# Final norm of a decoder block: tiles 0 and 2 scaled by ScalarE and GpSimd, tiles 1 and 3 by VectorE

## The chip, the cores and the metric

The kernel runs on one core of a Trainium2 chip. The metric is the device time of one execution in microseconds (us), the median of several runs. A core has five engines that run their own instruction streams and meet at semaphores: TensorE (PE in the profile, PEld its weight loads), VectorE (DVE), ScalarE (ACT), GpSimd (POOL) and SyncE (SP), which here only issues DMAs.

## The reference

One decoder layer over 512 tokens of width 1024: token mixers, a cross-attention, and a mixture of 32 experts of which each token uses two. Everything ahead of the last step is unchanged here. What matters is how the block ends:

```
for e in range(N_EXPERTS):
    gate, up = jnp.split(t @ w_gate_up[e], 2, axis=-1)
    y = (jax.nn.silu(gate) * up) @ w_down[e]
    out = out + combine[:, e:e + 1] * y
x = x + out
return x * lax.rsqrt(mean(x * x, axis=-1) + EPS) * final_norm
```

## The kernel before

The 512 tokens are four tiles of 128 rows (`NT = 4`), the 1024 columns lie in the free dimension. The experts run one after the other, bound by their weights and by TensorE. The rows of the first 30 experts are written to memory and gathered back by GpSimd (`gpsimd_last`, indirect DMAs into `y1` and `y2`); VectorE adds them, weighted, to the block's input (`rows_in`, lines 2464 and 2465, into `sums`). The last two experts don't take that way: TensorE adds their rows (`late_rows`, line 2448) and then `sums` (`own_rows`, line 2453) in PSUM. Tile t has PSUM banks 2t and 2t + 1, 512 columns each (`sum_banks`). All eight banks are in use then, and none is used again.

What follows, for each tile in turn, is the final norm, the subject of this case:

- ScalarE (`scalar_last`) squares both banks with a running sum (line 2491, one ACTIVATE and one short read of the accumulator for each bank), adds the two halves (line 2494), and takes Ln and Exp (lines 2496 and 2498): a first value `rf` of the root.
- VectorE (`vector_last`) waits for that value (semaphore `sq_done`), refines it in four small operations of one element per partition, each waiting for the one before (`newton`, lines 157 to 160), and then for each bank does `y2 = bank * rf * final_g` in one scalar_tensor_tensor (line 2481). After the second it raises `done`.
- SyncE (`sync_last`) waits for `done` tile by tile, in the order 0, 1, 2, 3, and issues one store of 512 KB for each (line 2442). At the end it waits for all four.

The final norm's weight `final_g`, spread over the partitions, was loaded long before. In the profile `final_g` and the squares' scratch have the name weights_2down, `y2` has the name weights_1lo, `y1` weights_0down and `sums` ring, since they reuse buffers of the weights. GpSimd has nothing to do after the last gather.

Of the kernel before, what the change touches and what calls it, by code (L numbers as in the profile page):

```python
# [10 lines left out]
ACT = mybir.ActivationFunctionType  # L11
AX = mybir.AxisListType

P = 128
SEQ, D, MEM = 512, 1024, 256
NT, MT, KC = SEQ // P, MEM // P, D // P
# [138 lines left out]
def newton(dve, st, r, a, mean, eps):  # L155

    st.link(dve.tensor_tensor(a, r, r, ALU.mult))
    st.link(dve.scalar_tensor_tensor(a, mean, eps, a, ALU.add, ALU.mult))  # L158
    st.link(dve.tensor_scalar(a, a, -0.5, 1.5, ALU.mult, ALU.add))  # L159
    st.link(dve.tensor_tensor(r, r, a, ALU.mult))  # L160
# [1688 lines left out]
def buffer_of(g, e, part):  # L1849

    return g["chunks"][chunk_at(e, part) % BUFFERS]
# [47 lines left out]
def expert_phase(nc, psum, g):  # L1899
# [6 lines left out]
    with ExitStack() as ctx:  # L1906
# [70 lines left out]
        with ExitStack() as inner:  # L1977
# [276 lines left out]

            summed = sem("rows_summed")
            last = finish_phase(nc, psum, g, locals(), inner)
            rows_in, sums = last["rows_in"], last["sums"]
            over = overflow_pass(nc, psum, g, locals(), inner)
# [130 lines left out]
def finish_phase(nc, psum, g, v, ctx):  # L2389

    x_rows, eps, R = g["x_rows"], g["eps"], g["routing"]
    y_dram, y_stored = v["y_dram"], v["stored"]

    def sb(name, shape, dt=F32):
        return ctx.enter_context(nc.sbuf_tensor(name, shape, dt))

    def sem(name):
        return ctx.enter_context(nc.semaphore(name))

    y1, y2 = buffer_of(g, NE - 3, "lo"), buffer_of(g, NE - 3, "hi")  # L2400
    sums = buffer_of(g, NE - 4, "down")
    spare = buffer_of(g, NE - 2, "lo")
    final_g, sqf = spare[:, 0], spare[:, 1]
    ss, lnf, rf, af = (sb(n, [P, NT]) for n in ("ss", "lnf", "rf", "af"))
    ss_half = sb("ss_half", [P, NT, 2])
    got = [sem(f"rows_back{t}") for t in range(NT)]
    summed = v["summed"]
    g_landed, sq_done, done, stored, pe_summed = (
        sem(n) for n in ("g_landed", "sq_done", "fin_done", "out_stored", "pe_summed"))
    EARLY_ROWS = NE - LATE  # L2410

    def sum_banks(t):
        return [psum[2 * t + n] for n in range(2)]

    def gpsimd_last(pool):
        def rows_of(table, rows):
            for t in range(NT):
                for y, row in zip((y1, y2), rows):
                    pool.indirect_dma_start(out=y[:, t, :], out_offset=None, in_=table,
                                            in_offset=bass.IndirectOffsetOnAxis(ap=row[:, t:t + 1], axis=0)  # L2420
                                            ).then_inc(got[t], 16)

        pool.wait_ge(v["longest_set"], 1)
        longest = pool.value_load(R["longest"][0:1, 0:1], min_val=0, max_val=SEQ - 1)
        pool.wait_ge(v["table_steps"], v["TABLE"])
        pool.wait_ge(v["gu_mm"], EARLY_ROWS)
        for q in range(2):
            pool.wait_ge(y_stored[q], 16 * (EARLY_ROWS // 2))
        rows_of(y_dram[:, :], (R["row_1"], R["row_2"]))
        with pool.If(longest >= SLOTS):  # L2430
            pool.wait_ge(v["over_stored"], 32 + 32 * (SEQ // SLOTS - 1) * NE)
            pool.wait_ge(summed, NT)
            rows_of(v["y_over"][:, :], v["over_row"])

    def final_gain(sp):
        sp.wait_ge(v["dn_mm"], EARLY_ROWS)
        sp.dma_start(final_g, g["final_norm"].partition_broadcast(P)).then_inc(g_landed, 16)

    def sync_last(sp):
        for t in range(NT):  # L2440
            sp.wait_ge(done, t + 1)
            sp.dma_start(g["out"][0].rearrange("(n p) d -> n p d", p=P)[t], y2[:, t]).then_inc(stored, 16)
        sp.wait_ge(stored, 16 * NT)

    def tensor_last(pe):
        def late_rows(t):
            for n, bank in enumerate(sum_banks(t)):
                pe.matmul(bank[:], v["late_turned"][n][:, t], v["late_yy"][n], start=True, stop=False)  # L2448

        def own_rows(t):  # L2450
            pe.wait_ge(summed, t + 1)
            for n, bank in enumerate(sum_banks(t)):
                pe.matmul(bank[:], g["ident"][:], sums[:, t, n * 512:(n + 1) * 512], start=False, stop=True).then_inc(pe_summed, 1)  # L2453
        pe.wait_ge(v["late_got"], 2 + LATE)
        pe.wait_ge(v["y_got"], NE)
        for t in range(NT):
            late_rows(t)
        for t in range(NT):
            own_rows(t)

    def rows_in(dve, k, weight, base, landed, signal):
        for t in range(NT):
            dve.wait_ge(got[t], landed)
            k.link(dve.scalar_tensor_tensor(y1[:, t], y1[:, t], weight[0][:, t:t + 1], base[:, t], ALU.mult, ALU.add))
            dve.scalar_tensor_tensor(sums[:, t], y2[:, t], weight[1][:, t:t + 1], y1[:, t], ALU.mult,
                                     ALU.add).then_inc(signal, 1)

    def early_rows(dve):
        dve.wait_ge(v["dn_mm"], NE - 3)
        rows_in(dve, Steps(dve, v["table_steps"], 1, v["TABLE"] + 1), v["early_weight"], x_rows, 32, summed)  # L2470

    def vector_last(dve):
        k = Steps(dve, v["table_steps"], 1, v["TABLE"] + 1 + NT)
        dve.wait_ge(g_landed, 16)
        for t in range(NT):
            dve.wait_ge(sq_done, 5 * t + 5)
            c = slice(t, t + 1)
            newton(dve, k, rf[:, c], af[:, c], ss[:, c], eps[:, 0:1])
            for n, bank in enumerate(sum_banks(t)):
                half = slice(n * 512, (n + 1) * 512)  # L2480
                last = dve.scalar_tensor_tensor(y2[:, t, half], bank[:], rf[:, c], final_g[:, half], ALU.mult, ALU.mult)  # L2481
            last.then_inc(done, 1)

    def scalar_last(act):
        act.wait_ge(v["dn_mm"], EARLY_ROWS)
        for t in range(NT):
            c = slice(t, t + 1)
            for n, bank in enumerate(sum_banks(t)):
                act.wait_ge(pe_summed, 2 * t + n + 1)

                act.activation(sqf[:, n * 512:(n + 1) * 512], bank[:], ACT.Square, scale=D ** -0.5,  # L2491
                               accum_out=ss_half[:, t, n:n + 1]).then_inc(sq_done, 1)
            act.wait_ge(sq_done, 5 * t + 2)
            act.activation(ss[:, c], ss_half[:, t, 0:1], ACT.Identity, bias=ss_half[:, t, 1:2]).then_inc(sq_done, 1)
            act.wait_ge(sq_done, 5 * t + 3)
            act.activation(lnf[:, c], ss[:, c], ACT.Ln, bias=eps[:, 0:1]).then_inc(sq_done, 1)
            act.wait_ge(sq_done, 5 * t + 4)
            act.activation(rf[:, c], lnf[:, c], ACT.Exp, scale=-0.5).then_inc(sq_done, 1)

    return dict(sync=sync_last, tensor=tensor_last, scalar=scalar_last, gpsimd=gpsimd_last, vector=vector_last,  # L2500
                final_gain=final_gain, early_rows=early_rows, rows_in=rows_in, sums=sums)

# [36 lines left out]
```

## Time and profile before

| | us |
|---|---|
| median of 3 runs | 1259.28 (1259.16 to 1260.41) |
| the profiled execution's own time | 1260.81 |
| its span, first to last instruction | 1259.1 |
| start of the first row sum that closes a bank (PE line 2453) | 1243.75 |
| start of the last store's issue | 1256.05 |

Times in rows are from the span's start. The span and the execution's own time differ by 1.7 us, which lies around the instructions. Busy times are shares of the whole span, though the change touches only its last 12 us or so.

### The profile page before, as it was taken

The numbers are of one execution on the slowest core, as the hardware profiler recorded it, in microseconds if no ns is written. First come the engines' busy times: TensorE is split into PE (matmuls) and PEld (weight loads), VectorE is DVE, ScalarE is ACT, GpSimd is POOL, SyncE is SP. The second block draws the span as 40 slices with busy tenths as digits, with TensorE's granted clock in tenths as the row PEclk, the third lists the DMA queues.
The fourth block names the chain that finished last, engine by engine and source line by source line (L and its number), as shares of the span: only waits on it lengthen the run. The fifth ranks groups of instructions, "written<-read, shape, count | busy, mean of one in ns | idle before, by whom it ended". The sixth has DMA issues, their size and how long they took to land. (4 is left out here: it accounts for less than half of the span.)

```text
span 1259.1 us, 18398 instructions
## 1 busy us (share of the span) xinstructions
PE 1232.0 (98%) x7153; PEld 857.5 (68%) x7153; DVE 678.6 (54%) x1228; ACT 384.9 (31%) x979; POOL 401.3 (32%) x431
## 2 busy tenths in 40 slices
PE   8999999999999999999999998999999999999996
PEld 6788989898888989878686786354444535353532
DVE  2744989999998998772534234321213122222126
ACT  2033745546373735522022231111111111111113
POOL 3266765757484753325411210000000000000002
PEclk9999999999999999999999998999999999999999
DMA  9672211221121212322334346889999999999995
GB/s 352 256 292 76 84 68 52 68 85 68 51 70 49 85 61 88 122 104 102 134 135 167 115 193 263 342 359 429 426 429 427 427 426 428 426 426 428 427 382 201
DMA packets 37302, 287.10 MB, mean 228 GB/s; under 512 B 6524, under 2 KB 6652, under 8 KB 23520
## 3 DMA queue, kind: packets, MB, share of 16 engines
q1 hardware_dynamic: 31488, 273.69, 53.9%
q0 software_dynamic: 3552, 8.20, 1.8%
q10 hardware_dynamic: 2176, 4.03, 0.9%
q8 instruction: 58, 0.95, 0.3%
q14 instruction: 28, 0.23, 0.0%
HBM read 269.84 MB, written 19.92 MB: 230 GB/s over the span
## 5 line engine op out<-in xcount | busy, mean ns | idle before, releaser
L2224 DVE TENSOR_SCALAR ee<-ee 128x256 f32<-128x256 f32 x32 | 9.4, 293 | 297.5 <-ACT ee L2121 297.5
L2200 POOL DMA_INDIRECT expert_out<-yy,row_at x30 | 29.4, 982 | 430.3 <-ACT yy L2105 430.3
L1942 PE MATMUL bank<-select,x_rows 128*128 128x256 f32 (+1 forms) x576 | 117.0, 363 | 2.8 <-DVE select L2210 2.8
L1942 PEld LDWEIGHTS bank<-select,x_rows 128*128 128x128 f32 x576 | 100.8, 196 | 21.0 <-issue 7.3
L704 PE MATMUL bank<-h_sums,ring 128*128 128x256 f32 x384 | 92.2, 383 | 0.0
L704 PEld LDWEIGHTS bank<-h_sums,ring 128*128 128x128 f32 x384 | 71.8, 190 | 10.0
L704 PE MATMUL bank<-h_sums,weights_0hi 128*128 128x256 f32 x256 | 60.5, 379 | 0.0
L704 PE MATMUL bank<-h_mix,weights_0lo 128*128 128x256 f32 x256 | 58.7, 382 | 1.4 <-PEq L176 1.4
L714 PE MATMUL bank<-weights_0lo,h_mix 128*128 128x128 f32 x512 | 59.2, 276 | 0.0
L2091 ACT ACTIVATE xg<-bank,cols 128x256 f32<-128x256 f32 (+1 forms) x72 | 28.1, 448 | 99.6 <-PE bank L1942 99.6
L714 PEld LDWEIGHTS bank<-weights_0lo,h_mix 128*128 128x128 f32 x512 | 57.9, 192 | 0.3
L2225 DVE RECIPROCAL ee<-ee 128x256 f32<-128x256 f32 x32 | 56.1, 1753 | 1.1
L704 PEld LDWEIGHTS bank<-h_mix,weights_0lo 128*128 128x128 f32 x256 | 47.9, 190 | 10.5 <-issue 4.4
L704 PEld LDWEIGHTS bank<-h_sums,weights_0hi 128*128 128x128 f32 x256 | 48.6, 190 | 6.6
L1660 DVE TENSOR_TENSOR x_t<-x_t,bank 128x256 f32<-128x256 f32 x42 | 17.7, 421 | 62.3 <-PE bank L1451 62.3
L2210 DVE TENSOR_SCALAR select<-slot_row,at_slot,root 128x64 f32<-128x64 f32 x128 | 29.3, 307 | 37.6 <-PE bank L1942 37.1
L909 ACT ACTIVATE ring<-bank 128x256 f32<-128x256 f32 x72 | 27.5, 382 | 69.2 <-PE bank L704 69.2
L675 POOL TENSOR_TENSOR dd<-bb 128x256 f32<-128x256 f32 x56 | 42.5, 760 | 14.7 <-DVE rr L1166 14.7
L2105 ACT ACTIVATE yy<-bank 128x512 f32<-128x512 f32 x30 | 17.9, 597 | 90.3 <-PE bank L1968 90.3
L704 PE MATMUL bank<-h_mix,ring 128*128 128x256 f32 x192 | 45.4, 379 | 0.0
L1961 ACT ACTIVATE ee<-bank 128x256 f32<-128x256 f32 x32 | 12.3, 384 | 103.8 <-PE bank L1957 103.7
L2121 ACT ACTIVATE ee<-bank 128x256 f32<-128x256 f32 x32 | 12.3, 384 | 100.5 <-PE bank L1951 100.5
(425 smaller groups left out, 2664.4 us busy)
## 6 DMA issues: line engine op xcount, KB each, us to landing
weights_0lo<-in_w_in SPq DMA_DIRECT2D x32, 512.0 KB, 4.3
weights_0lo<-in_w_gate_up SPq DMA_DIRECT2D x7, 2048.0 KB, 24.0
weights_1down<-in_w_gate_up SPq DMA_DIRECT2D x7, 2048.0 KB, 26.4
weights_0hi<-in_w_gate_up SPq DMA_DIRECT2D x7, 2048.0 KB, 25.0
weights_1hi<-in_w_gate_up SPq DMA_DIRECT2D x7, 2048.0 KB, 27.8
weights_0hi<-in_w_in SPq DMA_DIRECT2D x24, 512.0 KB, 4.0
kv_rows<-in_w_gate_up SPq DMA_DIRECT2D x6, 2048.0 KB, 16.9
weights_0down<-in_w_gate_up SPq DMA_DIRECT2D x6, 2048.0 KB, 18.4
```

Of the source, the lines that this page charges most:

```text
L675: pool.tensor_tensor(dk, ref, k1, ALU.subtract)
L704: mm = pe.matmul(bank[:, 0:HALF_T], w[:, k], h[:, k], start=(fresh and k == 0), stop=(k == HALF_K - 1), skip_group_check=True)
L714: mm = pe.matmul(bank[:, cs], h_mix[:, k, cs], ring[2][:, k], start=(k == 0), stop=(k == KC - 1))
L909: act.activation(dst, bank, ACT.Copy).then_inc(taken, 1)
L1660: dve.tensor_tensor(here, here, bank, ALU.add).then_inc(evac, 1)
L1942: mm = pe.matmul(bank[:, n * width:(n + 1) * width], x_rows[:, t, k * P:(k + 1) * P], sel[:, t, columns], start=(t == 0), stop=(t == NT - 1))
L1961: return act.activation(h_t[q].rearrange("p c h s -> p (c h s)"), bank[:, 0:2 * P], ACT.Copy)
L2091: act.activation(xg[:, k, first:first + width], bank[:, u * width:(u + 1) * width], ACT.Copy, scale=g["g_ffn"][:, k:k + 1]).then_inc(x_tak ...
L2105: act.activation(yy[q][:], Y[q][:], ACT.Copy).then_inc(y_got, 1)
L2200: pool.indirect_dma_start(out=half_rows, out_offset=bass.IndirectOffsetOnAxis(ap=row_at[:, e:e + 1], axis=0), in_=yy[e % 2][:], in_offset= ...
L2210: mark = dve.tensor_scalar(sel[:, t, column:column + SLOTS], g["slot_row"][:], R["at_slot"][:, t, e:e + 1], R["root"][:, t:t + 1], ALU.is_ ...
L2225: st.link(dve.reciprocal(ee[q][:], ee[q][:]))
```

## The change

Tiles 0 and 2 are finished by another pair of engines. After `newton`, VectorE copies their refined root into a small tile of its own, `r_pool`, raises `rooted`, and goes on to the next tile. ScalarE, once it has given the first root value of the next tile (1 or 3), copies the two banks of tile 0 or 2 from PSUM into `y2`, multiplied by `r_pool`. GpSimd, which now gets `gpsimd_gain` behind its gathers, waits for both copies (`by_root`) and multiplies the whole 128x1024 tile by `final_g`, in place. SyncE waits for GpSimd's semaphore for tiles 0 and 2 and for VectorE's for tiles 1 and 3; the order of the stores stays. Tiles 1 and 3 are computed as before.

```diff
     def gpsimd_last(pool):
...
+        gpsimd_gain(pool)
+
+    def gpsimd_gain(pool):
+        pool.wait_ge(g_landed, 16)
+        for t in range(0, NT, 2):
+            pool.wait_ge(by_root, t + 2)
+            pool.tensor_tensor(y2[:, t], y2[:, t], final_g, ALU.mult).then_inc(done_pool, 1)
 
     def sync_last(sp):
         for t in range(NT):
-            sp.wait_ge(done, t + 1)
+            sp.wait_ge(done if t % 2 else done_pool, t // 2 + 1)
             sp.dma_start(g["out"][0].rearrange("(n p) d -> n p d", p=P)[t], y2[:, t]).then_inc(stored, 16)
         sp.wait_ge(stored, 16 * NT)
...
             newton(dve, k, rf[:, c], af[:, c], ss[:, c], eps[:, 0:1])
+            if t % 2 == 0:
+                dve.tensor_copy(r_pool[:, c], rf[:, c]).then_inc(rooted, 1)
+                continue
             for n, bank in enumerate(sum_banks(t)):
...
             act.activation(rf[:, c], lnf[:, c], ACT.Exp, scale=-0.5).then_inc(sq_done, 1)
+            if t % 2:
+                act.wait_ge(rooted, t // 2 + 1)
+                for n, bank in enumerate(sum_banks(t - 1)):
+                    act.activation(y2[:, t - 1, n * 512:(n + 1) * 512], bank[:], ACT.Copy,
+                                   scale=r_pool[:, t - 1:t]).then_inc(by_root, 1)
```

## Rows read from the trace of the kernel before

**Rows 1.** The page, busy time of each engine: us, share of the span, instructions.

```profile
PE 1232.0 (98%) x7153; PEld 857.5 (68%) x7153; DVE 678.6 (54%) x1228; ACT 384.9 (31%) x979; POOL 401.3 (32%) x431
```

**Rows 2.** The chain that ended last, from 1215 us: start, us, what.

```profile
1243.91 1.73 PE bank L2453 x4
...
1254.62 0.75 DVE weights_1lo L2481
1255.37 0.66 DVEq L1977
```

**Rows 3.** Timeline, 1225 us on: start, us, engine, line, operation, idle before.

```profile
1243.75 7.03 PE L2453 MATMUL bank<-ring,ident 128*128 128x512 f32 x16
...
1247.04 0.20 ACT L2498 ACTIVATE rf<-lnf 128x1 f32<-128x1 f32 x1
...
1247.35 0.16 DVE L157 TENSOR_TENSOR af<-rf 128x1 f32<-128x1 f32 x1 [1.26 <-ACT rf L2498]
...
1248.17 1.41 DVE L2481 SCALAR_TENSOR_TENSOR weights_1lo<-bank,rf,weights_2down 128x512 f32<-128x512 f32 x2
...
1249.08 0.20 ACT L2498 ACTIVATE rf<-lnf 128x1 f32<-128x1 f32 x1
1249.19 0.58 ACT L2491 ACTIVATE weights_2down<-bank 128x512 f32<-128x512 f32 x1
...
1253.17 0.20 ACT L2498 ACTIVATE rf<-lnf 128x1 f32<-128x1 f32 x1
1253.79 0.15 DVE L157 TENSOR_TENSOR af<-rf 128x1 f32<-128x1 f32 x1
...
1254.62 1.41 DVE L2481 SCALAR_TENSOR_TENSOR weights_1lo<-bank,rf,weights_2down 128x512 f32<-128x512 f32 x2
```

**Rows 4.** Timeline of SyncE's queue from 1254.5 us: the last store's issue.

```profile
1256.05 0.33 SPq L2442 DMA_DIRECT2D out<-weights_1lo  x1
```

**Rows 5.** DMA issues from 1240 us: count, KB each, median us to landing.

```profile
out<-weights_1lo SPq DMA_DIRECT2D x4, 512.0 KB, 2.6
```

**Rows 6.** Windows at the end; the last three columns are PEclk, DMA share, GB/s.

```profile
1256.50:1257.00 0.50, 0.00 (x0) 0.00 (x0) 0.00 (x0) 0.00 (x0) 0.00 (x0) 0.50 0.29 115
...
1257.50:1258.00 0.50, 0.00 (x0) 0.00 (x0) 0.00 (x0) 0.00 (x0) 0.00 (x0) 0.50 0.99 401
1258.00:1258.25 0.25, 0.00 (x0) 0.00 (x0) 0.00 (x0) 0.00 (x0) 0.00 (x0) 0.50 0.67 262
```

**Rows 7.** ScalarE's groups by shape: busy us, mean ns, idle before.

```profile
L2105 ACT ACTIVATE yy<-bank 128x512 f32<-128x512 f32 x30 | 17.9, 597 | 90.3 <-PE bank L1968 90.3
...
L1053 ACT ACTIVATE dd<-bank,eps 128x512 f32<-128x512 f32 x8 | 5.5, 687 | 17.1 <-PE bank L870 17.1
```

**Rows 8.** GpSimd's groups by shape, the same columns.

```profile
L613 POOL TENSOR_TENSOR ring<-ring,weights_0hi 128x512 f32<-128x512 f32 x8 | 12.2, 1521 | 0.6
...
L327 POOL TENSOR_TENSOR h_sums<-h_mix 128x1024 f32<-128x1024 f32 x1 | 2.4, 2357 | 24.9 <-DVE h_mix L417 24.9
```

**Rows 9.** Timeline, 605 to 615 us: ScalarE hands a tile to GpSimd.

```profile
605.33 0.61 ACT L1593 ACTIVATE weights_2down<-x_t 128x512 f32<-128x512 f32 x1
...
606.02 1.27 POOL L1393 TENSOR_TENSOR weights_2down<-weights_2down 128x512 f32<-128x512 f32 x1 [9.09 <-ACT weights_2down L1593]
```

**Rows 10.** Timeline, 38 to 43 us: small VectorE operations beside GpSimd.

```profile
37.76 2.36 POOL L327 TENSOR_TENSOR h_sums<-h_mix 128x1024 f32<-128x1024 f32 x1 [24.93 <-DVE h_mix L417]
...
40.07 2.35 POOL L328 TENSOR_TENSOR h_sums<-h_mix 128x1024 f32<-128x1024 f32 x1
40.17 2.27 DVE L425 TENSOR_TENSOR lb<-lb_e 128x8 f32<-128x8 f32 x1
```

**Rows 11.** Timeline, 172 us: a VectorE operation with one PSUM input beside GpSimd.

```profile
172.24 0.75 DVE L158 SCALAR_TENSOR_TENSOR dd<-bank,eps,dd 128x512 f32<-128x512 f32 x1
172.48 0.73 POOL L624 TENSOR_TENSOR kv_rows<-kv_rows,ring 128x256 f32<-128x256 f32 x1 [2.64 <-ACT kv_rows L909]
```

More of the change, by code:

```diff
@@ L2404, in finish_phase @@
     ss, lnf, rf, af = (sb(n, [P, NT]) for n in ("ss", "lnf", "rf", "af"))
-    ss_half = sb("ss_half", [P, NT, 2])
+    ss_half, r_pool = sb("ss_half", [P, NT, 2]), sb("r_pool", [P, NT])
     got = [sem(f"rows_back{t}") for t in range(NT)]
     summed = v["summed"]
-    g_landed, sq_done, done, stored, pe_summed = (
-        sem(n) for n in ("g_landed", "sq_done", "fin_done", "out_stored", "pe_summed"))
+    g_landed, sq_done, done, stored, pe_summed, rooted, by_root = (
+        sem(n) for n in ("g_landed", "sq_done", "fin_done", "out_stored", "pe_summed", "fin_rooted", "fin_by_root"))
+    done_pool = sem("fin_done_pool")
     EARLY_ROWS = NE - LATE
```

## The prediction

> **What bounds the kernel now.** I read the page first. TensorE is busy for 98% of the span and no other engine for much over half of it [rows 1], so the kernel as a whole is a TensorE kernel. That says nothing about the change, which touches only what comes after TensorE's last work. So I went to the chain that ended last and to its end [rows 2]: TensorE holds it until the first banks are closed, at about 1245.6 us, and from there to 1256.03 it is on ScalarE for one tile and then on VectorE for four. Then I read the timeline of that stretch [rows 3], and the view by windows for the last 3 us [rows 6].
>
> The reader is to see two staggered conveyors. ScalarE gives the first root value of tile 0 at 1247.24 and of tile 1 at 1249.28, so it needs 2.04 us a tile, without a pause, and it gives tile 3's at 1253.37. VectorE starts tile 0 at 1247.35 and its line 2481 at 1248.17, so the four small operations take 0.82 us, 0.2 us each. Its two large operations take 1.41 us, and its period is (1253.79 - 1247.35) / 3 = 2.15 us. VectorE is the slower one, but by 0.11 us a tile only. It starts tile 3 at 1253.79, where it could have started at 1253.37 + 0.11 = 1253.48 (0.11 us is tile 0's gap from ScalarE's end to VectorE's start). **So 0.31 us is all that relief of VectorE can bring**, even if it cost the other engines nothing.
>
> The last store is issued at 1256.05 [rows 4], 0.02 us after VectorE's end. It lands after 2.6 us [rows 5], and the span ends 3.05 us after the issue. Its data runs at some 400 GB/s with the 16 DMA engines full, from within the window that starts at 1256.50 to within the one that ends at 1258.25: 0.29 x 0.5 + 1.0 + 0.67 x 0.25 = 1.3 us [rows 6], which is also 524 KB / 401 GB/s. Today the stores are issued 2.15 us apart, so each is through before the next begins.
>
> **The change part by part.**
>
> *Removed from VectorE:* four of eight line 2481 operations, 1.41 us for each of tiles 0 and 2. *Added there:* two copies of one element per partition, of a size with the small operations, 0.2 us each. VectorE now waits for ScalarE at tiles 1, 2 and 3. Tile 0's copied root is there at about 1248.17 + 0.2 = 1248.4, ScalarE asks for it at 1249.19, so that wait costs nothing. The wait for tile 2's root costs nothing either: its first value is there at 1252.56 (below), refined and copied by 1253.7, or by 1254.0 with the stall named below, and ScalarE asks at 1254.47.
>
> *Added on ScalarE, first pair.* Two PSUM reads of 128x512 with a scale from a [128,1] column. The nearest row with such an operand takes 687 ns, one without it 597 ns [rows 7]. I take the first. Consecutive operations here overlap: the exponential starts at 1249.08, lasts 0.20 us, and the next starts at 1249.19, so 0.09 us goes off. Two copies take 2 x (0.69 - 0.09) = 1.19 us. They stand ahead of tile 2's squares, in a stream that has no pause. TensorE gives no cover: its last bank is closed at 1250.78, before the squares need it. So all that ScalarE does for tiles 2 and 3 moves back 1.19 us, and tile 3's value comes at 1253.37 + 1.19 = 1254.56 instead of 1253.37. Bounds for the pair are 1.0 us (without the operand's cost) and 1.4 us (without overlap).
>
> *VectorE's tile 3* then starts at 1254.67, and ends at 1254.67 + 0.82 + 1.41 = 1256.90. That is 0.87 us later than today: the relief is already more than paid for, with GpSimd at no cost.
>
> *Added on ScalarE, second pair.* They start 0.11 us after the start of tile 3's exponential: 1253.17 + 1.19 + 0.11 = 1254.47, and end at 1254.47 + 0.60 + 0.69 = 1255.76.
>
> *Added on GpSimd.* The hand-over took 606.02 - 605.94 = 0.08 us [rows 9], so tile 2's multiplication starts at 1255.84. The profile has GpSimd operations of two inputs on this very shape, 128x1024 in float32, at 2.36 us, and half that size at 1.52 us on the mean of a group that shares time with VectorE [rows 8]. I take 2.35, the same shape without disturbance, and keep 2 x 1.52 = 3.04 as the upper bound. The rows of this shape are 2.36 and 2.35 [rows 8, 10], so nothing goes off below. The end is 1258.19. GpSimd has no other work then, and its first multiplication (tile 0, from about 1250.55 to 1252.9) lies in front of nothing.
>
> *The stores.* SyncE keeps the order. Tile 0's store goes out at 1252.9 and tile 1's right behind, both through by 1256.3, ahead of the others. Tile 2's goes out at 1258.20 (0.02 us after GpSimd), and tile 3's, whose rows were ready at 1256.90, is queued behind the wait for tile 2 and goes out 0.35 us later. So two stores of 1.3 us each are now side by side, and the last one ends 1.3 us after the first, by the row in which one store alone already fills the DMA engines [rows 6].
>
> *The sum.* Last free-standing issue 1256.05, now 1258.20: +2.15. The second store's data: +1.30. Together **+3.45 us**; the span goes from 1259.1 to 1262.5. The profiled execution would go from 1260.81 to 1264.3. It lies 1.5 us over the median of the runs; the difference is the same for both, so I add it to the median: 1259.28 + 3.45 = 1262.7 us. What can't be told from no change here is 0.2%, or 2.5 us.
>
> **The shared port.** In the rows, a small VectorE operation with its inputs in SBUF that starts beside a GpSimd operation lasts as long as that one: 2.27 us for 128x8 elements, ending with GpSimd at 42.4 [rows 10]. One with a PSUM input and one SBUF tile ran beside GpSimd undisturbed, 0.75 us, and GpSimd's on 128x256 elements took 0.73 [rows 11]. Here tile 2's refinement would start at 1252.67 inside GpSimd's first multiplication and be held for 0.2 to 0.3 us, which has 0.5 us of slack. Tile 3's refinement is over at 1255.49, 0.35 us before GpSimd's second starts, and line 2481 is of the undisturbed kind. So I cost it at nothing; if GpSimd started a little before 1255.49 instead, VectorE would stand until about 1257.8, finish tile 3 at about 1259.5, and its store would end the span at 1259.5 + 3.05 = 1262.5, the same by another way. The Trainium skill, page "SBUF — State Buffer", section "Who interferes with whom", says that VectorE operations with two SBUF inputs and GpSimd operations which read SBUF hold one port pair as a lock, while those with one SBUF input do not contend. Rows 10 and 11 fit it, and the sum by it is the one above. The Trainium skill, page "GPSIMD Engine Reference", section "Engine selection", speaks against the change: it advises VectorE for elementwise work, with 4497 against 2293 ns for 2048 elements of a two-input add. An estimate from that page is 2.25 us for 1024, where the row has 2.36; by it the sum would be +3.35.
>
> **The rivals.**
>
> *A. The two last stores overlap* (this one ends on the other side). If part of a store's time is a delay that the second can share, it costs its issue distance, 0.35 us, and the sum is 2.15 + 0.35 = +2.5 us, 1261.8: just within 0.2%. It decides from 0.37 us for the second store downwards. Against it: the DMA engines' share is 0.99 during one store [rows 6]. For it: 1.3 us of the 2.6 to landing are not data.
>
> *B. GpSimd's multiplication is stretched* to 3.04 us [rows 8], by its operands or by VectorE: +4.15 us, 1263.4.
>
> *C. Lock the other way:* GpSimd waits until VectorE has finished line 2481 at 1256.90 before it starts. That costs 1.06 us: +4.5 us, 1263.8. Against it stand rows 11.
>
> *D. VectorE's relief is what counts,* and GpSimd and ScalarE hide. At best that is -0.31 us, 1259.0, no change that can be told. It would need ScalarE's copies in a pause that the timeline doesn't have, and GpSimd's 2.35 us before 1256. Faster by more than 0.2% has no mechanism in the tail; only a shift of the 1245 us before it could give it. The runs before span 1.25 us.
>
> **How the numbers follow.** Forecast (+3.45 with its bounds) 0.62, A 0.14, B 0.11, C 0.06, D with all unnamed shifts 0.07. The bounds of the sum: ScalarE's two pairs 2 x 0.2 = 0.4 us either way, GpSimd +0.7, the second store -0.95. So it runs from 3.45 - 0.4 - 0.95 = +2.1 to 3.45 + 0.4 + 0.7 = +4.55, 1261.4 to 1263.8. This takes in A, B and C. With some of the spread of the runs on each side I give 1261.1 to 1264.2. The forecast lies 0.9 us over the bound of 0.2%, and the spread of the runs can bring it under: 0.12 of its 0.62. With most of A and part of D, within 0.2% gets 0.26; faster 0.04; slower 0.70.
>
> **What would show it.** In the profile after: line 2491's squares of tile 2 start 1.2 us later than 1249.19; ScalarE's copies last 0.69 us; GpSimd's two multiplications last 2.35 us each; VectorE idles before each `newton`; SyncE's wait ahead of tile 2's store ends with GpSimd at about 1258.2, and the last two issues lie 0.35 us apart; the DMA engines are full for 2.6 us at the end. The chain at the end runs ScalarE, GpSimd, DMA, with VectorE gone from it. The forecast is wrong if GpSimd's operation takes under 1.5 us, if the second store adds under 0.4, or if the start of the tail, 1243.75, moves by over a microsecond.

## The result and the profile after

| | before | after |
|---|---|---|
| median, 8 runs each | 1259.22 us (1258.63 to 1260.44) | 1263.07 us (1262.19 to 1263.86) |
| span of the profiled execution | 1259.1 | 1262.1 |
| first row sum that closes a bank (start) | 1243.75 | 1243.43 |
| from there to the end of the span | 15.35 | 18.67 |

The ratio is 1.0028, with a 95% interval of 1.0019 to 1.0037: slower by 3.5 us (2.4 to 4.7); the two medians lie 3.85 us apart. The work ahead of the tail moves by a microsecond or two from one execution to the next (its end lies between 1241.63 and 1244.15 us in the 13 traces of this study), so below the distance in the last row of the table, called **the tail**, is what runs are compared by. The change adds 3.3 us to it. Spans are given to 0.1 us, so a tail is good to about 0.1 us. Two kernels of this study were traced twice, and their tails came back within that: 17.77 and 17.78, 14.70 and 14.77.

The timeline of the changed kernel from 1243 us on (start, us, engine, line, operation, idle before and its releaser). It answers to [rows 3]; line 2492 is the former 2481, 2509 the former 2498, 2461 the former 2453.

```profile
1243.43 7.03 PE L2461 MATMUL bank<-ring,ident 128*128 128x512 f32 x16
...
1248.76 0.20 ACT L2509 ACTIVATE rf<-lnf 128x1 f32<-128x1 f32 x1
1248.87 1.25 ACT L2513 ACTIVATE weights_1lo<-bank,r_pool 128x512 f32<-128x512 f32 x2
...
1249.83 1.41 DVE L2492 SCALAR_TENSOR_TENSOR weights_1lo<-bank,rf,weights_2down 128x512 f32<-128x512 f32 x2
1250.01 0.59 ACT L2502 ACTIVATE weights_2down<-bank 128x512 f32<-128x512 f32 x1
1250.27 2.34 POOL L2441 TENSOR_TENSOR weights_1lo<-weights_1lo,weights_2down 128x1024 f32<-128x1024 f32 x1 [12.56 <-ACT weights_1lo L2513]
...
1252.19 0.44 DVE L157 TENSOR_TENSOR af<-rf 128x1 f32<-128x1 f32 x1 [0.96 <-ACT rf L2509]
...
1254.00 0.20 ACT L2509 ACTIVATE rf<-lnf 128x1 f32<-128x1 f32 x1
1254.11 1.25 ACT L2513 ACTIVATE weights_1lo<-bank,r_pool 128x512 f32<-128x512 f32 x2
1254.24 0.16 DVE L157 TENSOR_TENSOR af<-rf 128x1 f32<-128x1 f32 x1 [0.78 <-ACT rf L2509]
...
1255.07 1.41 DVE L2492 SCALAR_TENSOR_TENSOR weights_1lo<-bank,rf,weights_2down 128x512 f32<-128x512 f32 x2
1255.43 2.35 POOL L2441 TENSOR_TENSOR weights_1lo<-weights_1lo,weights_2down 128x1024 f32<-128x1024 f32 x1 [2.82 <-ACT weights_1lo L2513]
```

The reader is to see where the stream of ScalarE has its new piece: tile 2's squares start at 1250.01, not right behind the exponential at 1248.87, and the exponential of tile 3 ends 1254.20 - 1243.43 = 10.77 us into the tail, where it was 1253.37 - 1243.75 = 9.62 [rows 3]. VectorE idles 0.96 us before tile 2 and 0.78 before tile 3; it has its relief, and nothing to do with it. GpSimd ends at 1257.78. The chain that ended last shows the same (start, us, what):

```profile
1248.96 1.16 ACT weights_1lo L2513 x2
...
1250.27 2.34 POOL weights_1lo L2441
1252.62 2.78 issue
1255.40 2.38 POOLq L1977
```

Before, it ended in VectorE [rows 2]; now in GpSimd (POOLq is GpSimd's sequencer, here at the end of the block). The 2.78 us called issue are no work: in the timeline GpSimd idles there for 2.82 us until ScalarE's copy of tile 2 releases it. So the path to GpSimd's second multiplication runs through ScalarE, not through the first multiplication. Last, the stores: SyncE's queue from 1257.5 us, the second of its two issues by itself, and the windows at the end (the last three columns are PEclk, DMA share, GB/s).

```profile
1257.81 0.81 SPq L2450 DMA_DIRECT2D out<-weights_1lo  x2
```

```profile
1258.18 0.43 SPq L2450 DMA_DIRECT2D out<-weights_1lo  x1
```

```profile
1258.50:1259.00 0.50, 0.00 (x0) 0.00 (x0) 0.00 (x0) 0.00 (x0) 0.00 (x0) 0.50 0.80 319
...
1259.50:1260.00 0.50, 0.00 (x0) 0.00 (x0) 0.00 (x0) 0.00 (x0) 0.00 (x0) 0.50 1.02 410
...
1261.00:1261.25 0.25, 0.00 (x0) 0.00 (x0) 0.00 (x0) 0.00 (x0) 0.00 (x0) 0.50 0.85 328
```

Two stores are issued 0.37 us apart, as soon as GpSimd is done, and the DMA engines are full from about 1258.6 to 1261.21 us, 2.6 us without a break; in [rows 6] it is 1.3 us for one.

### The profile page after: what moved, and what is told of

Its sections match the earlier page's. It is cut to its first block and busy times, and to the rows that moved or that the text cites. A ratio compares the mean times of both kernels' runs of the same rounds, so it can differ in the third digit from the quotient of the medians.

```text
span 1262.1 us, 18403 instructions
## 1 busy us (share of the span) xinstructions
PE 1231.1 (98%) x7153; PEld 856.8 (68%) x7153; DVE 675.7 (54%) x1226; ACT 386.9 (31%) x983; POOL 405.4 (32%) x433
```

## The experiments

Each row is one trace; the tail is the span's end less the start of the first row sum. Ratios are against the kernel before on the same chip, with their 95% intervals.

| kernel | tail, us | against 15.35 | ratio of the times |
|---|---|---|---|
| before | 1259.1 - 1243.75 = 15.35 | | |
| changed | 1262.1 - 1243.43 = 18.67 | +3.3 | 1.0028 [1.0019, 1.0037] |
| e1, stores 0, 1, 3, 2 | 1259.4 - 1241.63 = 17.77 | +2.4 | 1.0023 [1.0013, 1.0033] |
| e8, the same again | 1261.2 - 1243.42 = 17.78 | +2.4 | one run |
| e2, tile 2 without GpSimd | 1259.6 - 1243.30 = 16.30 | +0.95 | 1.0011 [1.0002, 1.0020] |
| e3, VectorE's relief for nothing | 1258.3 - 1243.33 = 14.97 | -0.4 | 0.9998 [0.9989, 1.0007] |
| e4, tile 0 only | 1258.7 - 1242.26 = 16.44 | +1.1 | 1.0012 [1.0003, 1.0021] |
| e5, tile 2 only | 1260.7 - 1243.10 = 17.60 | +2.25 | 1.0017 [1.0008, 1.0027] |
| e6, last store in halves | 1258.2 - 1243.50 = 14.70 | -0.65 | 0.9996 [0.9987, 1.0005] |
| e10, the same again | 1258.2 - 1243.43 = 14.77 | -0.6 | 0.9994 [0.9985, 1.0003] |
| e7, changed, in halves | 1262.0 - 1244.15 = 17.85 | +2.5 | 1.0021 [1.0012, 1.0030] |
| e9, e7 with one wait more | 1261.2 - 1243.41 = 17.79 | +2.4 | 1.0017 [1.0008, 1.0026] |
| e11, before, idle GpSimd work | 1259.9 - 1242.84 = 17.06 | +1.7 | 1.0017 [1.0008, 1.0027] |

**e3: what is VectorE's relief worth?** The kernel before, with line 2481 left out for tiles 0 and 2.

```diff
             newton(dve, k, rf[:, c], af[:, c], ss[:, c], eps[:, 0:1])
+            if t % 2 == 0:
+                dve.tensor_copy(af[:, c], rf[:, c]).then_inc(done, 1)
+                continue
             for n, bank in enumerate(sum_banks(t)):
```

> The kernel before with line 2481 left out for tiles 0 and 2 (these rows aren't scaled; VectorE raises the semaphore after one small copy): VectorE's relief for nothing. Theory (VectorE is only 0.31 us late at tile 3): 15.0 us from the first row sum to the end, -0.3. Rival (VectorE's 2.8 us of work lie on the path): 12.5 us, -2.8.

The tail is 14.97 us, 0.4 less, and the times can't be told from those of before. 2.8 us of work were taken from VectorE (four operations of 0.7 us), and all but 0.4 of it became idle time. The rows at tile 3 (timeline) say why it is 0.4 and not 0.31:

```profile
1252.76 0.20 ACT L2501 ACTIVATE rf<-lnf 128x1 f32<-128x1 f32 x1
1252.99 0.16 DVE L157 TENSOR_TENSOR af<-rf 128x1 f32<-128x1 f32 x1 [0.96 <-ACT rf L2501]
```

VectorE starts 0.03 us after ScalarE's value, where the prediction had taken the 0.11 us of tile 0. So in the kernel before it was 1253.79 - 1253.37 - 0.03 = 0.39 us late, and its end moved by about that: 1255.23 - 1243.33 = 11.90 us into the tail, from 1256.03 - 1243.75 = 12.28. This is the ceiling of any plan that only moves this work elsewhere.

**e2: and with ScalarE's copies paid?** The changed kernel, tile 2's multiplication by the norm weight left out.

```diff
-        for t in range(0, NT, 2):
+        for t in (0,):
             pool.wait_ge(by_root, t + 2)
...
-            sp.wait_ge(done if t % 2 else done_pool, t // 2 + 1)
+            sp.wait_ge((done_pool, done, by_root, done)[t], (1, 1, 4, 2)[t])
```

> The changed kernel without GpSimd's multiplication of tile 2 by the norm weight (that part of the computation is left out); SyncE waits for ScalarE's copies instead. Theory (ScalarE's extra pair alone already costs more than VectorE's relief brings): tile 3 ends VectorE's work 0.8 us later than before, and its store is just clear of tile 2's: 16.2 to 16.3 us from the first row sum to the end, +0.9 against the kernel before. Rival (the whole loss is GpSimd's two-input operation, and VectorE's relief is a gain without it): 15.0 to 15.3 us, 0 to -0.3.

It gave 16.30, the number of the theory. The rival, that GpSimd is the whole loss, is out: without GpSimd on the path the tail is still 0.95 us longer than before. The rows divide it. Tile 3's store is issued 1256.38 - 1243.30 = 13.08 us into the tail, 0.78 later than before, since VectorE ends later. The other 0.17 lie behind the issue: the end comes 3.22 us after it instead of 3.05. In the windows the DMA engines are busy without a pause from 1253.3 to 1258.69 us, so tile 3's data probably still had tile 2's ahead of it: its store was not quite clear of tile 2's, which the theory had assumed.

**e5 and e4: one tile of the two.** e5 sends tile 2 alone by the new way, e4 tile 0 alone. In e5:

```diff
-        for t in range(0, NT, 2):
-            pool.wait_ge(by_root, t + 2)
+        for t in (2,):
+            pool.wait_ge(by_root, 2)
...
-            sp.wait_ge(done if t % 2 else done_pool, t // 2 + 1)
+            sp.wait_ge(*((done, 1), (done, 2), (done_pool, 1), (done, 3))[t])
...
-            if t % 2 == 0:
+            if t == 2:
...
-            if t % 2:
-                act.wait_ge(rooted, t // 2 + 1)
+            if t == 3:
+                act.wait_ge(rooted, 1)
```

e4 has the same edits for tile 0 (SyncE takes tile 0 from GpSimd and tiles 1 to 3 from VectorE; ScalarE copies in turn 1).

> Only tile 2 goes by ScalarE and GpSimd; tiles 0, 1 and 3 by VectorE; order of the stores kept. Theory: no pair stands ahead of the squares, so the copies of tile 2 start 9.5 us after the first row sum, GpSimd ends at 13.2, its store and tile 3's behind it end the span at 17.55 us, +2.2 against before; the difference of 1.1 us to the changed kernel is ScalarE's first pair. Rival (the delay comes from GpSimd and the stores alone, tile 0's part being harmless): as the changed kernel, 18.7 us, +3.3.

> Only tile 0 goes by ScalarE and GpSimd, tiles 1 to 3 by VectorE. Theory: ScalarE's pair moves the root of tile 3 back by 1.15 us, and since tile 2 is on VectorE again, the 0.25 us for which its first small operation stands behind GpSimd is on the path: VectorE ends 13.5 us after the first row sum, span end 16.6 us, +1.2 against before. Without the lock it would be 16.3 us, +1.0. Rival (GpSimd is the whole loss, and for tile 0 it is hidden): 15.35 us, 0.

e5 gave 17.60, and the difference to the changed kernel, 1.07 us, is the cost of ScalarE's first pair, which stands ahead of tile 2's squares. e4 gave 16.44: tile 0's part is not harmless, though nothing on the path waits for GpSimd's product. Its VectorE rows show the small stall of the shared port too (timeline; tile 2's first small operation, then tile 3's):

```profile
1251.03 0.44 DVE L157 TENSOR_TENSOR af<-rf 128x1 f32<-128x1 f32 x1 [0.96 <-ACT rf L2509]
...
1253.46 0.15 DVE L157 TENSOR_TENSOR af<-rf 128x1 f32<-128x1 f32 x1
...
1254.28 1.41 DVE L2492 SCALAR_TENSOR_TENSOR weights_1lo<-bank,rf,weights_2down 128x512 f32<-128x512 f32 x2
```

GpSimd ran from 1249.10 to 1251.45, and the operation of one element that began at 1251.03 ended at 1251.47, 0.28 us late. VectorE ended 1255.69 - 1242.26 = 13.43 us into the tail (13.5 expected).

**e1 and e8: the order of the stores.** The changed kernel with one edit, run twice for its trace.

```diff
-        for t in range(NT):
+        for t in (0, 1, 3, 2):
             sp.wait_ge(done if t % 2 else done_pool, t // 2 + 1)
```

> The changed kernel with the stores issued in the order 0, 1, 3, 2. Measured from the first start of the row sum that closes the banks to the end of the span, the kernel before takes 15.35 us and the changed one 18.67. Theory (the second store's data costs 1.3 us because it is queued behind GpSimd): tile 3 is issued about 13.1 us after that start and is through before tile 2's data begins, so only GpSimd's end counts: 17.4 us, +2.1 against the kernel before, 1.3 less than the changed kernel. Rival A (two stores share most of their time): only some 0.3 us less than the changed kernel, 18.3 us.

It gave 17.77. That is 0.9 less than the changed kernel, so rival A (0.3) is out, but 0.35 more than expected. The second trace was to say whether that is chance:

> The kernel with the stores in the order 0, 1, 3, 2 once more, for its trace. It took 17.75 us from the first row sum to the end where 17.4 were expected, and 0.6 us of SyncE's wait at the end came after the landing, 0.2 in the other traces. If that belongs to this order of stores, both numbers come back. If it is chance, the end is at 17.4 and the wait at 0.2.

It came back. In e8's windows (the first and the last with store data for tiles 3 and 2) the store data ran from about 1257.3 to 1259.92 us, 16.50 us into the tail at its end. In the changed kernel that was 1261.21 - 1243.43 = 17.78. So the data's end did move by 1.28 us, as forecast, and 0.4 of it was lost after it.

```profile
1257.00:1257.50 0.50, 0.00 (x0) 0.00 (x0) 0.00 (x0) 0.00 (x0) 0.50 (x1) 0.50 0.35 139
...
1259.50:1260.00 0.50, 0.00 (x0) 0.00 (x0) 0.00 (x0) 0.00 (x0) 0.00 (x0) 0.50 0.83 336
```

SyncE's waits in e8 (engine, line, waited for: us, times, longest) show it as the last row, which is 0.2 us before and in the changed kernel:

```profile
SPq L1977 <- DMA out<-weights_1lo: 2.3, 1, 2.3
SPq L1977 <- PEq L1977: 0.5, 1, 0.5
```

**e7: both terms made small.** GpSimd in halves behind each of ScalarE's copies, tile 2's store in halves around tile 3's.

```diff
-            pool.wait_ge(by_root, t + 2)
-            pool.tensor_tensor(y2[:, t], y2[:, t], final_g, ALU.mult).then_inc(done_pool, 1)
+            for n in range(2):
+                half = slice(n * 512, (n + 1) * 512)
+                pool.wait_ge(by_root, t + n + 1)
+                pool.tensor_tensor(y2[:, t, half], y2[:, t, half], final_g[:, half], ALU.mult).then_inc(done_pool, 1)
...
-        for t in range(NT):
-            sp.wait_ge(done if t % 2 else done_pool, t // 2 + 1)
-            sp.dma_start(g["out"][0].rearrange("(n p) d -> n p d", p=P)[t], y2[:, t]).then_inc(stored, 16)
+        lo, hi, all_of = slice(0, 512), slice(512, 1024), slice(0, D)
+        for t, s, value, cols in ((0, done_pool, 2, all_of), (1, done, 1, all_of), (2, done_pool, 3, lo),
+                                  (3, done, 2, all_of), (2, done_pool, 4, hi)):
+            sp.wait_ge(s, value)
+            sp.dma_start(g["out"][0].rearrange("(n p) d -> n p d", p=P)[t][:, cols], y2[:, t, cols]).then_inc(stored, 16)
-        sp.wait_ge(stored, 16 * NT)
+        sp.wait_ge(stored, 16 * (NT + 1))
```

> The changed kernel with both terms of the sum made small: GpSimd multiplies tiles 0 and 2 in halves of 512 columns, each as soon as ScalarE has copied it, and the stores go out as tile 0, tile 1, first half of tile 2, tile 3, second half of tile 2. Theory: tile 2's second half ends on GpSimd 13.9 us after the first row sum (14.35 in the changed kernel), and the DMA engines are busy from 13.45 without a pause until 16.05: 17.0 us to the end of the span, +1.65 against the kernel before. So even this form doesn't reach it, since ScalarE's first pair (1.15 us) stays. Rival (the loss is only in how the tail was put together, and the split of work itself is sound): 15.3 us or less, 0 or a gain.

It gave 17.85 instead of 17.0, a miss of 0.85 us. VectorE's rows of its timeline say why; GpSimd's row is from its own view.

```profile
1254.96 0.16 DVE L157 TENSOR_TENSOR af<-rf 128x1 f32<-128x1 f32 x1 [1.06 <-ACT rf L2513]
1255.15 0.22 DVE L158 SCALAR_TENSOR_TENSOR af<-ss,eps,af 128x1 f32<-128x1 f32 x1
1255.40 0.15 DVE L159 TENSOR_SCALAR af<-af 128x1 f32<-128x1 f32 x1
1255.59 1.26 DVE L160 TENSOR_TENSOR rf<-rf,af 128x1 f32<-128x1 f32 x1
1256.89 1.41 DVE L2496 SCALAR_TENSOR_TENSOR weights_1lo<-bank,rf,weights_2down 128x512 f32<-128x512 f32 x2
```

```profile
1255.58 2.49 POOL L2443 TENSOR_TENSOR weights_1lo<-weights_1lo,weights_2down 128x512 f32<-128x512 f32 x2 [2.67 <-ACT weights_1lo L2517]
```

GpSimd started 0.01 us before the fourth small operation, and that one, with two SBUF inputs of one element each, stood for 1.26 us until GpSimd's first half (1.26 us too) was done. Line 2496, with one PSUM and one SBUF tile, then ran beside the second half in its usual 1.41. The earlier start of GpSimd had hit VectorE's path. The 17.0 expected were out of reach even without that: GpSimd ends 1258.07 - 1244.15 = 13.92 us into the tail, and e11 below shows that the span ends no sooner than 3.4 us after it, at 17.3.

**e9: the same without that collision.** Only this is added to e7:

```diff
+            if t:
+                pool.wait_ge(rooted, 3)
             for n in range(2):
...
+            if t == NT - 1:
+                dve.tensor_copy(r_pool[:, c], rf[:, c]).then_inc(rooted, 1)
```

> The form in halves, with one wait more: GpSimd starts tile 2 only when VectorE has refined tile 3's root (one more copy of one element per partition signals it). In the form without that wait, line 160 for tile 3 lasted 1.26 us instead of 0.16, since GpSimd had started 0.01 us before it. Theory (that was the shared port): line 160 lasts 0.16 us again, VectorE ends at 13.2 us after the first row sum instead of 14.15, GpSimd later, at 14.35, and its store's data comes behind 2.6 us of stores from 13.95: 17.4 us to the end of the span, 0.4 less than the 17.85 without the wait. Rival (the delay was VectorE's own, or GpSimd's lateness costs as much): 17.85 us or more.

Tile 3's line 160 is back at 0.16 us, and VectorE ends 1256.53 - 1243.41 = 13.12 us into the tail (14.15 in e7, since 1256.89 + 1.41 - 1244.15 = 14.15). So the stall was GpSimd's doing. But the tail is 17.79, not 17.4: once more 0.4 us are missing. Here the windows show the last data at about 1260.08 - 1243.41 = 16.67 us, 0.1 later than the 16.55 of the theory, and the end 1.1 us after it where the changed kernel has 0.9; so 0.2 of it are lost after the last data.

**e11: GpSimd's own end.** e1, e8 and e9 have one thing in common: the span ends 1259.4 - 1255.99 = 3.41, 1261.2 - 1257.77 = 3.43 and 1261.2 - 1257.78 = 3.42 us after GpSimd's last operation. To separate that from the stores, the kernel before got a GpSimd operation on which nothing depends.

```diff
+    idle_done = sem("idle_done")
...
+        pool.wait_ge(done, NT)
+        pool.tensor_tensor(y1[:, 0, 0:512], y1[:, 0, 0:512], y1[:, 1, 0:512], ALU.mult).then_inc(idle_done, 1)
```

> The kernel before, with one GpSimd multiplication of 128x512 on scratch rows added behind VectorE's last operation; nothing waits for it and no store depends on it. In three traces with the last store released by GpSimd (the stores in the order 0, 1, 3, 2 twice, and the halves with one wait more) the span ended 3.41 to 3.43 us after GpSimd's last operation, whatever the stores did. Theory (GpSimd's end is followed by 3.4 us of its own before the span can end): it ends 13.65 us after the first row sum, and the span at 17.05, +1.7 against before, with the last store landed long before. Rival (the 3.4 us were the stores'): 15.35 us, as before.

The tail is 17.06. These are GpSimd's row of its timeline, and SyncE's waits (the queue named as releaser in the last one, PEq, is inferred):

```profile
1255.21 1.26 POOL L2436 TENSOR_TENSOR weights_0down<-weights_0down 128x512 f32<-128x512 f32 x1 [17.55 <-DVE weights_1lo L2484]
```

```profile
SPq L1977 <- DMA out<-weights_1lo: 2.3, 1, 2.3
SPq L1977 <- PEq L1977: 1.9, 1, 1.9
```

The last store was issued at 1255.16 and had landed after its usual 2.3 us of waiting; then SyncE stood for 1.9 us more, and the span ended at 1259.9, 3.43 us after GpSimd's 1256.47. So GpSimd's last operation sets a floor of its own under the end of the span. It counts from the operation's end and not from the release of GpSimd's wait: that was 4.7 us before the end of the span here, and 5.8 in e8. In the changed kernel, e5 and e7 the span ends 4.3, 4.3 and 3.9 us after GpSimd's last operation, so there the stores end it.

**e6 and e10: a better kernel before?** The rows say that the end is a delay plus data, so half of the last store can go while VectorE does its last half.

```diff
-        for t in range(NT):
+        for t in range(NT - 1):
...
-        sp.wait_ge(stored, 16 * NT)
+        for n in range(2):
+            sp.wait_ge(done, NT + n)
+            half = slice(n * 512, (n + 1) * 512)
+            sp.dma_start(g["out"][0].rearrange("(n p) d -> n p d", p=P)[NT - 1][:, half], y2[:, NT - 1, half]).then_inc(stored, 16)
+        sp.wait_ge(stored, 16 * (NT + 1))
...
-            last.then_inc(done, 1)
+                if t == NT - 1 or n:
+                    last.then_inc(done, 1)
```

> The kernel before with tile 3's store cut into two of 512 columns each, the first issued after the first of the two line 2481 operations. Theory (the end is a fixed delay plus data at 400 GB/s): the data of the last store is half, 0.65 us, and the first half is through by then: 14.65 to 14.7 us from the first row sum to the end, -0.7 against before. Rival (a store costs by its rows and not by its bytes, so each half takes 1.3 us): 15.9 us, +0.5.

> The kernel before with tile 3's store in two halves once more, since 0.7 us is about what 11 runs on each side can tell. Theory: 14.7 us from the first row sum to the end again (15.35 before), and a median 0.3 to 0.7 us under the kernel before. Rival (the trace's gain is given back elsewhere): a ratio of 1.0000 or more.

14.70 and 14.77 us: the trace has the gain, 0.6 us, twice. The medians were 1259.46 against 1259.75 and 1259.06 against 1259.95. Both point the same way, and both intervals take in 1, so this is a version that the trace calls better and the measured times have not confirmed. It is the only one here that is not worse than the kernel before by its trace and computes the whole.

## Why the prediction was right, point by point

The forecast was +3.45 us, 1262.7, in a range of 1261.1 to 1264.2. The measured median is 1263.07; the ratio gives +3.5 us, the tail of the traces +3.3. That 3.5 and 3.45 agree to 0.1 us is in part luck, since the ratio's interval runs from 2.4 to 4.7. The step from span to median did not hold either: the profiled execution lay 1.5 us over the median before, but 1263.86 - 1263.07 = 0.8 over it after, so the two medians differ by 3.85 where the two profiled executions differ by 3.05.

- **VectorE is only 0.31 us late:** e3 took 2.8 us of work from it and gained 0.4. It was 0.39 us late, since from tile 1 on VectorE starts 0.03 to 0.04 us after ScalarE's value and not tile 0's 0.11.
- **ScalarE's first pair, +1.19 on everything behind it:** 1.15 in the trace (10.77 against 9.62 us into the tail), and 1.07 between the changed kernel and e5. The copies last 673 ns on the mean, taken as 690. The page row with the column operand was the right neighbour.
- **VectorE's tile 3 ends 0.87 us later though it was relieved:** in the trace 1256.48 - 1243.43 = 13.05 against 1256.03 - 1243.75 = 12.28, so 0.77. The 0.1 less is the shorter hand-over (0.04 instead of 0.11) and ScalarE's 1.15 instead of 1.19. e2 shows the effect on the end: 0.78 of its +0.95.
- **GpSimd 2.35 us for 128x1024:** 2.34 and 2.35. The prediction's estimate of 2.25, from the Trainium skill, page "GPSIMD Engine Reference" (its two figures stand there in the section "Elementwise — side-by-side cycle accounting"), is 0.09 us low here. Rival B (3.04) is out, and so is rival C: it started at 1255.43 while VectorE's line 2492 had been running since 1255.07, and neither was longer than usual.
- **The shared port:** tile 2's first small operation lasted 0.44 us instead of 0.16, within the slack, as said. The failure named beside it, GpSimd starting a little early and VectorE standing on the path, did not happen in the changed kernel by 0.4 us (the last small operation ended at 1255.03, GpSimd began at 1255.43), and happened in e7: there VectorE stood for one half of GpSimd's work, 1.26 us, and not for the whole that the prediction priced. The rule of the Trainium skill, page "SBUF — State Buffer", section "Who interferes with whom", is borne out on both sides here: two SBUF inputs wait (1.26 us), one beside a PSUM input does not (1.41 as ever). But one SBUF input alone is not safe. The page excepts VectorE's 2-port modes, which the prediction left out, and names tensor_scalar among the operations that can enter them. The stretch of [rows 10] has such a case, a tensor_scalar of 128x8 with one SBUF input that stood for 2.27 us behind GpSimd's 2.34; which mode it ran in, no row shows:

```profile
42.37 2.34 POOL L330 TENSOR_TENSOR h_sums<-h_mix,h_sums 128x1024 f32<-128x1024 f32 x1
42.47 2.27 DVE L428 TENSOR_SCALAR pack<-cols 128x8 f32<-128x8 f32 x1
```

- **The issue that GpSimd releases, 2.15 us after the last one of before:** 1257.81 - 1243.43 = 14.38 against 1256.05 - 1243.75 = 12.30, so 2.08.
- **The second store's 1.30 us of data:** the DMA engines were full for 2.6 us, with the issues 0.37 us apart (0.35 forecast). Rival A is out by that row, and by the data's end in e8.
- **One thing was missing from the sum,** and that its result took no harm is luck: the floor under GpSimd's end. In the changed kernel it lies at 14.35 + 3.42 = 17.77 us into the tail, and the stores end it at 18.67. So of the 1.30 us of the second store only 0.9 is net, as e1 and e8 show; had it cost nothing at all, the tail would still have been +2.4 us. The price of rival A, +2.5, would have been near that by accident.

The sum of the terms as measured is 2.08 + 1.30 = 3.4, against 3.3 from the spans. Nothing in the traces has to be explained by the work ahead of the tail.

What stays open is what GpSimd does in its 3.4 us. The profile shows only that SyncE waits at the end of the block, on line 1977, after its last store has landed.

## What to carry to other kernels

An engine that is busy to the end of the chain is worth relieving only by as much as it lags behind the one that feeds it: lay the two cadences side by side (here 2.04 and 2.15 us a tile), and see what the feeder is charged for the relief. Work that is put into a stream without a pause moves all that stands behind it in that stream; the same copies cost the roots of tiles 0 and 1 nothing, and those of tiles 2 and 3 1.15 us. And at the end of a kernel stores want to be spaced: two that become ready together cost the data time of the second (1.3 us here, 0.9 of it net), which no engine's row shows.

## What the runs showed of the hardware beyond that

- After GpSimd's last elementwise operation the span did not end for another 3.41 to 3.43 us, in four traces with different stores (e1, e8, e9, e11; spans to 0.1 us). After VectorE's last it was 3.07 us before, and 1258.2 - 1255.78 = 2.42 in e6, so VectorE's end has no such floor. A GpSimd operation on which nothing depends lengthened the tail by 1.7 us, and the time by a ratio of 1.0017 [1.0008, 1.0027].
- An operation of one element per partition with two SBUF inputs on VectorE took 0.16 us alone and 1.26 us when GpSimd had begun 0.01 us earlier.
- A 512 KB store, issued at 0, has its data on the DMA engines from about 0.8 to 2.1 us and lands at 2.6. Cut in two of 256 KB with 2 KB runs it kept its rate, some 380 GB/s, and the tail became 0.6 us shorter (e6, e10).
